# A two-layer hybrid decoder trunk on one core: zeros multiplied ahead of the first unit, later loads, and a split last unit and last store

## What is computed

```python
D_MODEL, SEQ, DEPTH = 2048, 256, 2
def reference(x, positions, ln_g, w_in, w_out, ...):
    for l in range(DEPTH):
        h = _rmsnorm(x, ln_g[l])
        u = h @ w_in[l]                      # 256 x 2048 times 2048 x 6232
        (g_a, g_b, g_c, g_d, a_q, a_k, a_v, a_lr, b_xbc, b_dt,
         c_q, c_kv, c_kr, d_q, d_k, d_v) = _split(u, IN_WIDTHS)
        log_a = log_sigmoid(a_lr @ gla_gate_w2[l] + gla_gate_b[l]) / 16
        y_a = _gla(a_q, a_k, a_v, log_a, gla_norm_g[l]) * silu(g_a)
        y_b = _ssd_mixer(b_xbc, b_dt, g_b, ...)
        y_c = _mla(c_q, c_kv, c_kr, positions, ..., w_uq, w_ukv, ...) * silu(g_c)
        dq, dk = (_rope(_rmsnorm(v), positions) for v in (d_q, d_k))
        y_d = _dilated_attention(dq, dk, d_v) * silu(g_d)
        x = x + concatenate([y_a, y_b, y_c, y_d]) @ w_out[l]   # 256 x 2048 times 2048 x 2048
    return x
```

## Time and profile before

| | |
|---|---|
| median of 3 runs | 855.07 us (854.78 to 856.03) |
| the profiled execution: device time | 853.81 us |
| its span, first to last instruction | 851.8 us |
| PE busy | 839.1 us, 99% |
| DVE busy | 522.7 us, 61% |
| ACT busy | 470.9 us, 55% |
| POOL busy | 61.7 us, 7% |
| DMA | 151.00 MB, mean 177 GB/s |

### The profile page before, as it was taken

The page is one execution under the profiler, slowest core; times in us unless marked ns, Lnnn a source line. Parts: engine busy times, 40 slices in busy tenths (PEclk is TensorE's granted clock), DMA queues, the critical chain, the costliest instruction groups (busy, mean ns, idle before and its releaser), DMA issues.

```text
span 851.8 us, 11406 instructions
## 1 busy us (share of the span) xinstructions
PE 839.1 (99%) x4384; PEld 709.9 (83%) x4384; DVE 522.7 (61%) x868; ACT 470.9 (55%) x782; POOL 61.7 (7%) x88
## 2 busy tenths in 40 slices
PE   6999999999999999999999999999999999999998
PEld 5778888998987888888888878889989888888886
DVE  5536874685696566544664477638838965655542
ACT  6556442874855665533455565448558665663331
POOL 1830000000300000000003000001002000000000
PEclk9999999999999999999999999999999999999999
DMA  9886553463655445656648745526536544546663
GB/s 337 312 274 205 174 176 112 114 206 95 196 179 158 139 134 162 193 189 191 187 164 261 249 139 182 174 79 185 149 99 196 176 146 145 170 131 218 194 187 115
DMA packets 46518, 151.00 MB, mean 177 GB/s; under 512 B 5712, under 2 KB 5824, under 8 KB 46208
## 3 DMA queue, kind: packets, MB, share of 16 engines
q1 hardware_dynamic: 43872, 141.71, 53.0%
q0 software_dynamic: 1984, 6.12, 2.8%
q10 hardware_dynamic: 608, 2.43, 0.7%
HBM read 148.13 MB, written 2.11 MB: 176 GB/s over the span
## 4 chain that ended last, share of the span: by engine, by line
PE 96%; DMA 2%; DVE 1%; ACT 0%; SPq 0%; issue 0%; DVEq 0%; ACTq 0%
PE gemm L564 27%; PE gemm L566 27%; PE gemm L565 27%; DMA raw<-in_weights_dram 2%; PE pairs L741 2%; PE pairs L643 1%; PE pairs L767 1%; PE pairs L756 1%; PE pairs L588 1%; PE pairs L748 1%; PE pairs L782 1%; DVE w_lo L1259 0%; PE pairs L795 0%; PE pairs L721 0%; PE pairs L720 0%; PE pairs L794 0%
## 5 line engine op out<-in xcount | busy, mean ns | idle before, releaser
L1259 DVE TENSOR_TENSOR w_lo<-raw,w_hi 128x1024 fp32r<-128x1024 f32 (+1 forms) x287 | 318.4, 1117 | 240.6 <-ACT w_hi L910 239.6
L564 PE MATMUL gemm<-w_hi,a_hi 128*128 128x512 f32 (+1 forms) x1148 | 432.8, 377 | 1.9 <-DVE w_lo L1259 1.9
L566 PE MATMUL gemm<-w_hi,a_lo 128*128 128x512 f32 (+1 forms) x1148 | 422.4, 368 | 0.0
L565 PE MATMUL gemm<-w_lo,a_hi 128*128 128x512 f32 (+1 forms) x1148 | 421.5, 367 | 0.0
L910 ACT ACTIVATE w_hi<-raw 128x1024 fp32r<-128x1024 f32 (+1 forms) x287 | 274.3, 969 | 188.8 <-PE gemm L566 157.7
L564 PEld LDWEIGHTS gemm<-w_hi,a_hi 128*128 128x128 f32 x1148 | 215.8, 188 | 38.9 <-DVE w_lo L1259 3.1
L566 PEld LDWEIGHTS gemm<-w_hi,a_lo 128*128 128x128 f32 x1148 | 215.6, 188 | 35.6
L565 PEld LDWEIGHTS gemm<-w_lo,a_hi 128*128 128x128 f32 x1148 | 216.2, 188 | 33.5 <-issue 1.0
L940 ACT ACTIVATE u<-gemm,st 128x512 f32<-128x512 f32 (+1 forms) x40 | 22.0, 603 | 19.5 <-PE gemm L566 19.5
L481 POOL TENSOR_TENSOR st<-st,powers 128x4 f32<-128x4 f32 (+2 forms) x8 | 2.1, 262 | 420.8 <-ACT arena L999 224.1
L1115 ACT ACTIVATE arena<-arena,st 128x128 f32<-128x128 f32 (+1 forms) x32 | 13.1, 444 | 28.2 <-DVE st L1473 28.2
(11 more groups left out here) (208 smaller groups left out, 634.5 us busy)
## 6 DMA issues: line engine op xcount, KB each, us to landing
raw<-in_weights_dram SPq DMA_DIRECT2D x223, 512.0 KB, 4.1
raw<-in_weights_dram SPq DMA_DIRECT2D x64, 278.0 KB, 2.9
wuq<-in_mla_w_uq_dram POOLq DMA_DIRECT2D x2, 1152.0 KB, 12.4
x<-in_x_dram SPq DMA_DIRECT2D x4, 512.0 KB, 10.2
o<-ssd_rows ACTq DMA_DIRECT2D x2, 1024.0 KB, 5.8
u<-in_xT_dram SPq DMA_DIRECT2D x3, 512.0 KB, 8.6
out_dram<-x SPq DMA_DIRECT2D x3, 512.0 KB, 6.7
wukv<-in_mla_w_ukv_dram POOLq DMA_DIRECT2D x2, 512.0 KB, 15.6
```

What stands on the lines that cost most here:

```text
L564: pe.matmul(acc_t[t], a_hi[:, k, tok[t]], hi, start=k == 0, stop=False)
L565: pe.matmul(acc_t[t], a_hi[:, k, tok[t]], lo, start=False, stop=False)
L566: last = pe.matmul(acc_t[t], a_lo[:, k, tok[t]], hi, start=False, stop=k == KT - 1)
L1259: TT(w_lo[:, n % SPLIT, 0:c], raw[:, n % RAW, 0:c], w_hi[:, n % SPLIT, 0:c].bitcast(F32), ALU.subtract).then_inc(split_done, 1)
```

## The change

Five edits.
- DVE fills 512 columns of the scratch area `arena` with zeros as its first act, and PE multiplies them three times (`WARM = 3`, plain float32, into `pairs`) before unit 0.
- The four parts of `x` are issued behind units 6 to 9 in place of 4 to 7; POOL issues `cst` and `lmask` when the last part of `x` has landed, in place of the last part of `xT0`. `x_stats` stands behind units 12 and 13 in both layers, `evac 0` at 14 in place of 12, `gla qk` at 16 in place of 13, and `gla q`, `gla k` behind `evac 1` on ACT.
- `wuq` and `wukv` are issued behind `gla rs` on POOL, with a semaphore of their own (`mla_in`) for which `mla_q` waits; the other stages wait for the small parameters alone.
- In the very last unit PE does all of token tile 0 and then all of tile 1, with a semaphore (`last_tile`) between; DVE adds tile 0 then.
- DVE adds tile 1 in two halves of 256 columns; the first half is stored from ACT's queue, the second from SP's, tile 0 from SP's.

```diff
--- before.py
+++ after.py
@@ -100,6 +100,8 @@
 PIECES = [[(0, 1), (1, 2)] + [(k, k + 2) for k in range(2, KT, 2)]] + [[(k, k + 4) for k in range(0, KT, 4)]] * (DEPTH - 1)
 PIECE_BASE = [sum(map(len, PIECES[:l])) for l in range(DEPTH + 1)]
 
+WARM = 3
+
 LEVELS = (64, 32, 16, 8, 4, 2, 1)
 NEG = -1e30
 
@@ -150,7 +152,7 @@
 
 
 
-PE_AT = {"gla qk": 13, "gla lr": 19, "gla z": 21, "gla G": 23}
+PE_AT = {"gla qk": 16, "gla lr": 19, "gla z": 21, "gla G": 23}
 for _n in range(8):
     PE_AT[f"gla level {_n}"] = 26 + 2 * _n
 PE_AT |= {"gla diag": 42, "ssd xT 0": 43, "ssd xT 1": 44, "gla out": 45, "ssd cum": 50, "ssd CB": 56,
@@ -176,7 +178,10 @@
 JOBS = list(PE_AT)
 
 X_NEXT = {UNITS - 6: 0, UNITS - 4: 1}
-EVAC_AT = {(b + 1) * UPB + 2: b for b in range(1, N_INB)} | {12: 0}
+EVAC_AT = {(b + 1) * UPB + 2: b for b in range(1, N_INB)} | {14: 0}
+
+X_LOAD = [6, 7, 8, 9]
+X_STATS = [12, 13]
 
 
 ORDER = {
...
-        "x rs sum, evac 0, gla q, gla k, evac 1, gla lr, gla abs, gla exp, gla ln, evac 2, gla G, gla E 0, gla E 1, "
+        "x rs sum, evac 0, evac 1, gla q, gla k, gla lr, gla abs, gla exp, gla ln, evac 2, gla G, gla E 0, gla E 1, "
@@ -359,12 +364,13 @@
 
 
 
-        cols_in, small_in, gate_in, params_in, out_written = (
-            sem(k) for k in ("cols_in", "small_in", "gate_in", "params_in", "out_written"))
+        cols_in, small_in, gate_in, params_in, mla_in, out_written = (
+            sem(k) for k in ("cols_in", "small_in", "gate_in", "params_in", "mla_in", "out_written"))
         XT_PARTS = ((0, 2), (2, 4), (4, 8), (8, 12), (12, 16))
         xT_in = [sem(f"xT_in_{c}") for c in range(len(XT_PARTS))]
         x_in = [sem(f"x_in_{c}") for c in range(4)]
-        first_in, first_hi, first_lo = sem("first_in"), sem("first_hi"), sem("first_lo")
+        first_in, first_hi, first_lo, last_tile = sem("first_in"), sem("first_hi"), sem("first_lo"), sem("last_tile")
+        warm = sem("warm")
         setup_chain = sem("setup_chain")
         x_updated = sem("x_updated")
         row_out, row_in = sem("row_out"), sem("row_in")
@@ -404,7 +410,17 @@
         def piece_of(l, k):
             return [k0 <= k < k1 for k0, k1 in PIECES[l]].index(True)
 
-        N_PARAMS = len(PARAM_WIDTHS) + 2
+
+        OUT_PARTS = [(c * WB, (c + 1) * WB, 0, T) for c in range(D // WB - 1)]
+        OUT_PARTS += [(D - WB, D, 0, 1), (D - WB, D - WB // 2, 1, 2), (D - WB // 2, D, 1, 2)]
+        LAST_BY_ACT = len(OUT_PARTS) - 2
+
+        def out_store(engine, i):
+            c0, c1, t0, t1 = OUT_PARTS[i]
+            engine.wait_ge(x_updated, updated(DEPTH - 1, 0) + i)
+            engine.dma_start(out_d.rearrange("o (t p) n -> p (o t) n", p=P)[:, t0:t1, c0:c1], x[:, t0:t1, c0:c1]).then_inc(out_written, 16)
+
+        N_PARAMS = len(PARAM_WIDTHS)
 
 
         @block.sync
@@ -422,22 +438,22 @@
                         sp.dma_start(raw[:, n % RAW, 0:UK * w], weights(l, n)).then_inc(weights_in[n % RAW], 16)
                     if l == 0 and n < len(XT_PARTS) - 1:
                         xT_load(sp, n + 1)
-                    if l == 0 and 4 <= n < 8:
-                        t, c = (n - 4) // 2, slice(n % 2 * D // 2, (n % 2 + 1) * D // 2)
-                        sp.dma_start(x[:, t, c], x_d.rearrange("o (t p) n -> p (o t) n", p=P)[:, t, c]).then_inc(x_in[n - 4], 16)
-
-            parts = [(c * WB, (c + 1) * WB, 0, T) for c in range(D // WB - 1)] + [(D - WB, D, t, t + 1) for t in range(T)]
-            for i, (c0, c1, t0, t1) in enumerate(parts):
-                sp.wait_ge(x_updated, updated(DEPTH - 1, 0) + i)
-                sp.dma_start(out_d.rearrange("o (t p) n -> p (o t) n", p=P)[:, t0:t1, c0:c1], x[:, t0:t1, c0:c1]).then_inc(out_written, 16)
-            sp.wait_ge(out_written, 16 * len(parts))
+                    if l == 0 and n in X_LOAD:
+                        i = X_LOAD.index(n)
+                        t, c = i // 2, slice(i % 2 * D // 2, (i % 2 + 1) * D // 2)
+                        sp.dma_start(x[:, t, c], x_d.rearrange("o (t p) n -> p (o t) n", p=P)[:, t, c]).then_inc(x_in[i], 16)
+
+            for i in range(len(OUT_PARTS)):
+                if i != LAST_BY_ACT:
+                    out_store(sp, i)
+            sp.wait_ge(out_written, 16 * len(OUT_PARTS))
 
 
         @block.gpsimd
         def _(pool):
             pool.dma_start(posi[:, :], pos_d.rearrange("o (t p) -> p (o t)", p=P), allow_slow_non_contiguous=True).then_inc(small_in, 16)
 
-            pool.wait_ge(xT_in[4], 16)
+            pool.wait_ge(x_in[3], 16)
             pool.dma_start(cst[:, :], consts_d).then_inc(small_in, 16)
             pool.dma_start(lmask[:, :, :].rearrange("p a b -> p (a b)"), masks_d).then_inc(small_in, 16)
             pool.memset(eps, EPS)
@@ -490,9 +506,9 @@
                 for k, src in (("gla_ng", gla_ng), ("ssd_ng", ssd_ng), ("q_ng", q_ng), ("kv_ng", kv_ng), ("q_hg", q_hg),
                                ("k_hg", k_hg), ("dq_g", dq_g), ("dk_g", dk_g), ("dtb", dt_bias), ("alog", A_log), ("D", D_d)):
                     pool.dma_start(param[k], src[l].partition_broadcast(P)).then_inc(params_in, 16)
-                pool.dma_start(wuq[:, :, :], w_uq[l].rearrange("(k p) n -> p k n", p=P)).then_inc(params_in, 16)
-                pool.dma_start(wukv[:, :], w_ukv[l]).then_inc(params_in, 16)
                 rsqrt("gla rs", grs, gss)
+                pool.dma_start(wuq[:, :, :], w_uq[l].rearrange("(k p) n -> p k n", p=P)).then_inc(mla_in, 16)
+                pool.dma_start(wukv[:, :], w_ukv[l]).then_inc(mla_in, 16)
                 rsqrt("mla crs", crs, css)
                 rsqrt("mla rs 0", mrs[:, 0:8], mss[:, 0:8])
                 rsqrt("mla rs 1", mrs[:, 8:16], mss[:, 8:16])
@@ -506,6 +522,10 @@
         @block.tensor
         def _(pe):
             pe.sem_inc(unit_used, SPLIT)
+
+            pe.wait_ge(warm, 1)
+            for i in range(WARM):
+                pe.matmul(pair[:, 0, 0, :], A(0, P), A(0, WB), start=True, stop=True)
             def xT(j, l):
 
                 pe.wait_ge(x_updated, updated(l - 1, j))
@@ -538,6 +558,18 @@
                         pe.wait_ge(split_done, l * UNITS + n + 1 + RAW)
                     if U_OUT <= n < U_OUT + UPB and n % 2 == 0:
                         pe.wait_ge(*dve(f"yT {(n - U_OUT) // 2}"))
+                    if (l, n) == (DEPTH - 1, UNITS - 1):
+
+                        for t in range(T):
+                            acc_t, tok = acc_ps[:, b % 2, t, 0:w], slice(t * P, (t + 1) * P)
+                            for j in range(UK):
+                                k = k0 + j
+                                hi, lo = (m[:, n % SPLIT, j * w:(j + 1) * w] for m in (w_hi, w_lo))
+                                pe.matmul(acc_t, a_hi[:, k, tok], hi, start=False, stop=False)
+                                pe.matmul(acc_t, a_hi[:, k, tok], lo, start=False, stop=False)
+                                last = pe.matmul(acc_t, a_lo[:, k, tok], hi, start=False, stop=k == KT - 1)
+                            last.then_inc(unit_used if t == T - 1 else last_tile, 1)
+                        return
                     for j in range(UK):
                         k = k0 + j
                         hi, lo = (m[:, n % SPLIT, j * w:(j + 1) * w] for m in (w_hi, w_lo))
@@ -734,7 +766,7 @@
                 def mla_q(t):
 
                     pe.wait_ge(*act("mla cT"))
-                    pe.wait_ge(params_in, (l + 1) * 16 * N_PARAMS)
+                    pe.wait_ge(mla_in, (l + 1) * 16 * 2)
                     ps = bank()
                     for half, (c, w) in enumerate(((0, 512), (512, 256))):
                         for k in range(3):
@@ -1126,8 +1158,8 @@
                         xT_hi(n + 2, 0)
                     if l and n in (0, 3, 5):
                         xT_hi((n + 2) // 2, l)
-                    if n in (8, 9):
-                        x_stats(n - 8)
+                    if n in X_STATS:
+                        x_stats(X_STATS.index(n))
                     if n == 13:
                         act_.preload_act_table_set("natural_log_exp_and_others")
                     for j in range(4):
@@ -1211,10 +1243,12 @@
                         ssd_sq()
                     if l + 1 < DEPTH and n == UNITS - 3:
                         xT_hi(0, l + 1)
+            out_store(act_, LAST_BY_ACT)
 
 
         @block.vector
         def _(v):
+            v.memset(A(0, WB), 0.0).then_inc(warm, 1)
             v.sem_inc(split_done, RAW)
 
             v.wait_ge(cols_in, 16)
@@ -1608,8 +1642,14 @@
                     if l + 1 < DEPTH and n == UNITS - 3:
                         xT_lo(0, l + 1)
 
-            for t in range(T):
-                x_update(3, 1, DEPTH * UNITS, slice(t, t + 1))
+            c = D - WB
+            v.wait_ge(last_tile, 1)
+            v.tensor_tensor(x[:, 0, c:], x[:, 0, c:], acc_ps[:, 1, 0], ALU.add).then_inc(x_updated, 1)
+            v.wait_ge(unit_used, DEPTH * UNITS + SPLIT)
+            for i in range(2):
```

(3 more changed lines are left out.)

## The result

The changed kernel takes 859.74 us (median of 6 runs, 858.27 to 863.19) against 855.51 us of the kernel before (median of 6, 854.78 to 857.86): a ratio of 1.0055, 95% interval 1.0041 to 1.0068. It is slower by 4.2 us. The forecast was 856.3, with 853.0 to 859.6 as range: the time lies 0.1 us above it. The profiled execution took 859.39 us, its span 857.6. The profiled execution of the kernel before took 853.81 us, less than any of its six timed ones, so that the two traces lie 5.8 us apart and the medians 4.2.

A forecast was written before the change was run, and what follows sets the result against it. PE was taken as the bound, busy 839.1 of 851.8 us. Span 851.8 - 1.28 - 1.20 + 4.3 - 0.6 = 853.0, plus 2.0 around it and 1.3 to the median, gave 856.3 us, range 853.0 to 859.6.

The forecast's parts named there:

- The gap before unit 6 goes, -1.28 us: PE's wait for unit 6's weights disappears because x is loaded behind units 6 to 9: -1.28 us.
- The constants are issued at 27.85: POOL issues the constants when the last part of x lands, at 27.85, 12.5 us later than at 15.36.
- Load 7.6 us: From POOL's issue of the constants to its first chain step: 7.6 us, bounds 6.3 to 8.3.
- Chain 12.2 us: POOL's angle chain: 11 us clear of DVE plus 1.2 of waits, 12.2 us, bounds 11 and 16.9.
- Two loads and `x rs` 2.1: On POOL behind the chain, two small loads and `x rs` add 2.1 us, so `x rs` is ready at 49.8.
- 3.95 us from `x rs` to the second matmul of unit 15: Moving two tiles, both splits and hand-over take 3.95 us, so `x rs` is needed by 45.5.
- Stall: PE waits before unit 15 because `x rs` comes late: +4.3 us in place of the earlier 1.20.
- `wuq`, `wukv` at 0: Moving these loads behind `gla rs` (unit 48), needed at unit 67, taken as 0, bounds 0 to +1.2 us.
- The end, -0.6 us: After PE's last matmul, earlier addition of tile 0 and a halved last store save 0.6 us, bounds 0 to -0.9.
- Zeros 0: Zeros before unit 0 speed its matmuls, but unit 1 still waits for DVE: 0, bounds -1.1 to +0.5 us.
- POOL is in time: Rival: constants sooner or a shorter chain shrink the stall before unit 15; 851.9 to 853.9 us, chance 0.16.
- chain as slow as before: Rival: POOL's slow steps or longer load put `x rs` at 55.1, stall 9.6, time 861.6 us; chance 0.12.

The follow-up runs named there:

- e8_xlater: Kernel before with only x behind units 6 to 9 and its stages moved later, constants loaded as early as before: 852.57 against 855.09 us, ratio 0.9968.
- e9_after_nomla: Changed kernel with wuq and wukv issued ahead of gla rs again, own semaphore kept: 858.17 us against 854.86 of the kernel before, ratio 1.0034.
- e12_nomla_again: Changed kernel with wuq and wukv issued ahead of gla rs again, a repeat as comparison: 858.07 us against 854.93 of the kernel before, ratio 1.0044.
- e3_mla: Kernel before with only the loads of wuq and wukv moved behind gla rs: 856.64 against 855.09 us, ratio 1.0015.
- e7_best: Changed kernel with constants early and wuq and wukv where they were, zeros kept: 850.77 us against 854.93 of the kernel before, ratio 0.9953.
- e1_tail: Kernel before with only the split of the last unit and of the last store: 854.40 against 855.09 us, ratio 0.9995.
- e2_zeros: Kernel before with only the three multiplications of zeros: 855.09 against 855.09 us, ratio 1.0002.
- e5_xrs_first: Changed kernel, constants still late, with x rs ahead of the 18 angle steps on POOL: 852.79 us against 854.86 of the kernel before, ratio 0.9973.
- e4_early: Changed kernel with POOL issuing the constants behind the last part of xT0, as before: 852.40 us against 854.86 of the kernel before, ratio 0.9966.
- e10_later_tail: Kernel before with x and its stages later and the split tail, no zeros: 851.73 us against 854.93 of the kernel before, ratio 0.9962.

## Why the prediction was wrong

The main mechanism was right (POOL's late chain, `x rs`, one stall before unit 15), and the time came out 3.0 us too low against the kernel before (+1.2 forecast, +4.2 measured), outside the range by 0.1. What failed are two prices put at nothing and one that was too small: the slow matmuls behind the stall had no term (1.5 us in the trace), the moved loads of `wuq` and `wukv` were taken as 0 (2.0 us), and the stall was forecast as 4.3 us (5.4). By the prediction's own steps:

- *The gap before unit 6 goes, -1.28 us*: right. No gap from 11.41 to 49.40, and e8_xlater gives 2.5 us for both gaps (for the split between them see there).
- *The constants are issued at 27.85*: 28.50, of which about 0.35 is a start that was later as a whole (unit 1 at 11.41 in place of 11.04) and 0.3 the time from a landing (28.20) to POOL's issue, which the kernel before has too (15.06 to 15.36). The queue model, parcels of 512 KB at 1.28 us in order of issue, holds.
- *Load 7.6 us*: 7.9. *Chain 12.2 us*: 36.41 to 49.14 is 12.7. The multiplication clear of DVE took 0.85 us against the 0.7 to 0.8 that I had taken. Two steps of the chain met a split of DVE, one of 64 columns (1.25 us in place of 0.45) and one of the three multiplications (1.40 in place of 0.85). That is 1.35 us, where I had added 1.2; the rest of the chain took 11.4, where I had 11. One argument for it was wrong: the last step's 0.40 us against 1.93 compares two forms, and the last step is short by its form (see the last section). *Two loads and `x rs` 2.1*: 2.1. Together `x rs` was done at 51.22 in place of 49.8.
- *3.95 us from `x rs` to the second matmul of unit 15*: 55.26 - 51.22 = 4.04. **Stall**: without a gap that matmul would stand at 11.75 + 14 x 2.72 = 49.83, so 5.4 us in place of 4.3. This term was sized 1.1 us too low, inside its bounds: `x rs` came 1.4 us later than forecast and PE 0.3.
- **The step that is missing**: a stall of PE was priced by its length alone. I had read in unit 0 that PE runs at 1.2 GHz after standing idle, used it for the zeros, and did not apply it to the 4.3 us of idleness that I forecast myself. It costs 1.5 us in the trace, and 2.0 in those of e9_after_nomla and e12_nomla_again. The Trainium skill, page "TensorE: Matmul & The Clock Gate", Part 1, warns of idle gaps between bursts of matmuls for this very reason, and the trace agrees: the gap of 5.05 us was followed by the slow pace, the two of about 1 us were not.
- **`wuq`, `wukv` at 0**: wrong, and it was the value that failed and not the bounds. I argued that the kernel before has no gap there and left it at that. The loads go out at 163.7 us, into the narrow units, which use up a transfer of 278 KB in 1.5 us, while ACT and DVE have stages in between. The weights of unit 54 landed 6.5 us after their issue, where it took 2.8 in the kernel before, and ACT waited for them. First ACT's split of unit 54 in the changed kernel, then with the loads back:

```profile
172.83 0.67 ACT L942 ACTIVATE w_hi<-raw 128x556 fp32r<-128x556 f32 x1 [2.27 <-DMA raw<-in_weights_dram]
```

```profile
171.74 0.67 ACT L942 ACTIVATE w_hi<-raw 128x556 fp32r<-128x556 f32 x1 [0.63 <-ACT st L1073]
```

In the trace it cost 1.6 us at the first layer (0.4 of them at the small gap, which is not shown to be the loads') and the rest of 1.96 at the second; by the runs 0.9 (e9_after_nomla) and 1.5 us (e3_mla). What lies "19 units ahead of use" was the wrong question: the loads were in time, but those who share the DMA engines with them were not. The DMA share, the last number but one, shows how much busier the DMA engines were. In 165 to 170 us it is 0.92 in the changed kernel, 0.41 with the loads back:

```profile
165.00:170.00 5.00, 5.00 (x39) 4.37 (x38) 5.00 (x13) 2.40 (x5) 0.10 (x1) 1.00 0.92 310
```

```profile
165.00:170.00 5.00, 5.00 (x39) 4.38 (x37) 5.00 (x14) 2.96 (x6) 0.00 (x0) 1.00 0.41 108
```

- *The end, -0.6 us*: 0.9 in the traces, 0.7 in the runs. The halved last store gave a little more.
- *Zeros 0*: right for the kernel before (1.0002), and for the reason given. They ended at 6.93 us, later than the 6.5 that I had allowed; that it cost nothing is luck, since the first weights landed later in that execution and their split was done at 6.93 too. What I did not see is that the zeros could pay once no landing sets unit 6; that they do is not shown (e7_best).

In sum, by the trace: a start of PE later by 0.4, stall +1.1, clock +1.5, the two loads +2.0, against -0.3 at the end, make 4.7 where the span was forecast 4.6 us too low (853.0 for 857.6). The medians moved 1.6 us less than the traces, since the trace that the forecast started from was a fast one; e1_tail and e2_zeros, with their second gap of 1.6 us, show 1.0 of that. The rival "POOL is in time" was far off. The rival "chain as slow as before" was not the case either, though its time, 861.6, was nearer to 859.74 than the forecast was.

## What to carry over

When one transfer is moved back to make room, look at what stands *behind* its wait in the order of the issuing engine: here one step of two small instructions that needed none of the data held up every weight split. Either move that step ahead (e5_xrs_first) or leave the transfer early (e4_early); both turned +4.2 us into -2.1 and -2.5. Price a stall of TensorE of several microseconds with the slow matmuls behind it (1.5 to 2.0 us behind stalls of 5.05 to 6.70 here, nothing behind gaps of up to 1.63), and a moved load by who shares the DMA engines at the new place, not only by when its own data is wanted.

## What the runs showed of the hardware that was not expected

- A step on POOL with two operations was shorter than one with a single operation, with DVE idle beside all of them. In the changed kernel's trace the 256-column step with two (minimum, then maximum, line 490) took 0.40 us, the same size with one multiplication (line 486) 0.85; at 128 columns it is 0.30 with two (multiply, then add, line 482) and 0.54 with one addition (line 488). The three multiplications of the chain might therefore be cheaper with a second, idle operation; it was not tried, and the cause is not shown.
- The time at which the lower clock ends at the start varies between executions: without zeros PE's steps in unit 0 went from 0.43 to 0.23 us at 9.9 us in the kernel before and at 10.6, 11.4 and 11.7 in e10_later_tail, e8_xlater and e1_tail, and in e3_mla not before unit 1, which started at 12.24. The instructions of PE, ACT and DVE are the same up to there.
